# Five fp32 query/key blocks instead of four between the softmax steps of a fused encoder layer, and a new slot plan for its small products

## What is computed

```python
fox_q, fox_k, fox_v, logf, mla_q, ckv, kr = project_mixers(h, pos, w_in, b_f, g_cq, w_uq, g_ckv)
fox_o = attend(fox_q, fox_k, fox_v, ..., FOX_SCALE, 1, cum, cum)     # group A, frame-causal
mk, mv = mla_keys_values(ckv, kr, w_ukv)
mla_o = attend(mla_q, mk, mv, ..., MLA_SCALE, CHUNK)                 # group B, chunk-causal
mixed = concat([rms_norm(fox_o, g_fox_out), rms_norm(mla_o, g_mla_out)])
x = x + mixed @ w_o
x = x + cross_attention(rms_norm(x, g_mem), mem_k, mem_v) @ w_mo     # 4 heads, 256 memory tokens
x = x + (silu(hf @ w_gate) * (hf @ w_up)) @ w_down                   # hidden 2816
```

## Time and profile before

| what | value |
|---|---|
| median of 3 runs | 945.84 us (945.76 to 948.37) |
| the profiled execution | 946.38 us, its span 944.6 us |
| PE busy | 881.9 us, 93% of the span, 6186 matmuls |
| PEld busy | 839.0 us, 89% |
| DVE, ACT, POOL busy | 393.7, 382.4, 383.0 us |
| DMA | 75.46 MB, mean 80 GB/s |
| chain that ended last | PE 67%, of it L371 21%, L372 20%, L373 20% |

### The profile page before, as it was taken

One profiled execution on the slowest core, in us unless ns is written; L12 is line 12 of the kernel. 1 busy time (PEld: TensorE's weight loads), 2 busy tenths in 40 slices (PEclk: granted clock), 3 DMA queues, 4 the chain that ended last, 5 costly groups with the idle time before them and its releaser, 6 DMA issues.

```text
span 944.6 us, 15579 instructions
## 1 busy us (share of the span) xinstructions
PE 881.9 (93%) x6186; PEld 839.0 (89%) x6186; DVE 393.7 (42%) x629; ACT 382.4 (40%) x686; POOL 383.0 (41%) x195
## 2 busy tenths in 40 slices
PE   6999999889999899898798999999999998999995
PEld 6988988778888899787698999999999998999994
DVE  5255555566667755934475221222222220211213
ACT  6343565566778434455353323332322331211210
POOL 5365963535325354752033434334334432433410
PEclk9999999789999999999899999999999998999997
DMA  7333321000113233340031332232232232223202
GB/s 232 112 100 126 99 79 53 23 0 19 45 60 132 90 94 113 90 129 23 1 90 46 112 89 70 86 87 68 89 89 78 77 83 62 85 78 85 84 17 101
DMA packets 25092, 75.46 MB, mean 80 GB/s; under 512 B 2880, under 2 KB 5000, under 8 KB 24904
## 3 DMA queue, kind: packets, MB, share of 16 engines
q1 hardware_dynamic: 25040, 74.74, 26.2%
HBM read 68.20 MB, written 6.53 MB: 79 GB/s over the span
## 4 chain that ended last, share of the span: by engine, by line
PE 67%; DVE 6%; issue 4%; ACT 4%; POOL 1%; DMA 0%; DVEq 0%; ACTq 0%
PE ps L371 21%; PE ps L372 20%; PE ps L373 20%; PE ps L534 2%; PE ps L517 1%; PE ps L543 1%; PE ps L389 1%; DVE sqacc L1556 1%; DVE small L1405 1%; PE ps L397 1%; DVE ptlo L1410 1%; DVE xb L1677 1%; DVE hlo L1549 1%; ACT hhi L867 1%; POOL wlo L1688 1%
## 5 line engine op out<-in xcount | busy, mean ns | idle before, releaser
L371 PE MATMUL ps<-hhi,whi 128*128 128x288 f32 x1120 | 336.5, 300 | 19.2 <-POOL wlo L1688 9.4
L372 PE MATMUL ps<-hhi,wlo 128*128 128x288 f32 x1120 | 333.5, 298 | 0.0
L373 PE MATMUL ps<-hlo,whi 128*128 128x288 f32 x1120 | 332.9, 297 | 0.0
L1827 POOL TENSOR_TENSOR wlo<-wraw,whi 128x1024 fp32r<-128x1024 f32 (+1 forms) x68 | 161.2, 2372 | 268.8 <-ACT whi L867 268.8
L371 PEld LDWEIGHTS ps<-hhi,whi 128*128 128x128 f32 x1120 | 213.5, 191 | 21.9 <-POOL wlo L1688 9.1
L372 PEld LDWEIGHTS ps<-hhi,wlo 128*128 128x128 f32 x1120 | 212.2, 189 | 0.1
L373 PEld LDWEIGHTS ps<-hlo,whi 128*128 128x128 f32 x1120 | 212.1, 189 | 0.0
L1688 POOL TENSOR_TENSOR wlo<-wraw,whi 128x1024 fp32r<-128x1024 f32 (+1 forms) x49 | 119.5, 2445 | 201.7 <-ACT whi L867 201.3
L867 ACT ACTIVATE whi<-wraw 128x1024 fp32r<-128x1024 f32 (+1 forms) x117 | 119.2, 1023 | 137.1 <-PE ps L373 123.1
L371 PE MATMUL ps<-hidhi,whi 128*128 128x288 f32 x352 | 105.3, 299 | 3.4 <-DVE hidlo L1663 3.4
L372 PE MATMUL ps<-hidhi,wlo 128*128 128x288 f32 x352 | 105.1, 299 | 0.0
(11 more groups left out here) (238 smaller groups left out, 1468.3 us busy)
## 6 DMA issues: line engine op xcount, KB each, us to landing
wraw<-w_ff SPq DMA_DIRECT2D x44, 512.0 KB, 3.5
wraw<-w_front SPq DMA_DIRECT2D x41, 512.0 KB, 3.6
wraw<-w_down SPq DMA_DIRECT2D x16, 512.0 KB, 3.6
wraw<-w_front SPq DMA_DIRECT2D x8, 384.0 KB, 3.5
wraw<-w_down SPq DMA_DIRECT2D x8, 384.0 KB, 3.2
xs<-x_t SPq DMA_DIRECT2D x8, 288.0 KB, 5.7
xa<-x_t SPq DMA_DIRECT2D x8, 288.0 KB, 5.2
out_y<-xb SPq DMA_DIRECT2D x8, 288.0 KB, 2.3
```

The costliest lines, as they stand in the source:

```text
L371: nc.tensor.matmul(out, lh, rh, start=start, stop=False)
L372: nc.tensor.matmul(out, ll, rh, start=False, stop=False)
L373: return nc.tensor.matmul(out, lh, rl, start=False, stop=stop)
L1827: g.tensor_tensor(ffw(c, 1, 1, n)[:, 0, :], wraw[:, c % 2, 0:n], f(ffw(c, 0, 1, n)[:, 0, :]), ALU.subtract)\
```

## The change

The block K1 leaves the stretch before the loop: the loop there makes three blocks (Q0, K0, Q1), and `QK_AT` has ten entries instead of eight, so that slots 0 to 19 all carry 12 matmuls of a query/key block (before, slots 0 to 7 and 11 to 18). Everything that follows K1's place moves with it: its eviction, the casts and low parts of heads 2 and 3 (from slots 0 to 3 to slots 5 and 6), the loads of past keys, and which filler frees which weight block (`FILLER_END`). `joined(c)` moves from slot 5c + 9 to slot 5c + 10. The latent pieces are given new slots in `UQ_AT`, `KP_AT` and `V_AT`, the transposes in `RB_AT`, and the tables of ACT, DVE and POOL follow them. POOL's copies of the tables, which change alike, are left out here.

```diff
@@ -49,13 +49,13 @@
-QK_AT = (1, 3, 5, 7, 12, 14, 16, 18)
-UQ_AT = (24, 34, 43, 45, 49, 56, 60, 69)
-KP_AT = (30, 40, 51, 62)
-V_AT = ((28, 29, 32, 33, 38, 39, 42), (54, 55, 58, 59, 64, 65, 66))
-RB_AT = (22, 26, 36, 47, 67, 73, 79, 85)
+QK_AT = (1, 3, 5, 7, 9, 11, 13, 15, 17, 19)
+UQ_AT = (23, 34, 42, 44, 49, 56, 62, 66)
+KP_AT = (29, 39, 51, 60)
+V_AT = ((25, 26, 31, 32, 33, 36, 41), (46, 54, 55, 58, 59, 64, 65))
+RB_AT = (21, 27, 37, 47, 68, 72, 79, 85)
...
-FR_AT = 71
+FR_AT = 70
@@ -67,7 +67,7 @@
-FILLER_END = {15: QK_AT[1], 16: QK_AT[3], 17: QK_AT[5], 18: QK_AT[7], 19: UQ_AT[1] + 1, 20: V_AT[0][6], 21: UQ_AT[3] + 1, 22: UQ_AT[5] + 1, 23: V_AT[1][6],
+FILLER_END = {14: QK_AT[1], 15: QK_AT[3], 16: QK_AT[5], 17: QK_AT[7], 18: QK_AT[9], 19: UQ_AT[1] + 1, 20: V_AT[0][6], 21: UQ_AT[3] + 1, 22: UQ_AT[5] + 1, 23: V_AT[1][6],
@@ -461,11 +461,11 @@
-            for i in range(4):
+            for i in range(3):
...
-                    pe.wait_ge(s_vev, (2, 4, 5)[i - 1])
+                    pe.wait_ge(s_vev, (2, 4)[i - 1])
@@ -523,7 +523,7 @@
-                    pe.wait_ge(s_qkev, 4)
+                    pe.wait_ge(s_vev, 5)
@@ -554,7 +554,7 @@
-                b, half = B_QK + 4 + i // 2, i % 2
+                b, half = B_QK + 3 + i // 2, i % 2
@@ -565,7 +565,7 @@
-                    pe.wait_ge(f_lo, B_QK + 4 + i // 2 + 1)
+                    pe.wait_ge(f_lo, B_QK + 3 + i // 2 + 1)
@@ -950,17 +950,17 @@
-                    act.wait_ge(s_fev, nth(QK_AT[4 * (c // 2) - 7]) + 1)
+                    act.wait_ge(s_fev, nth(QK_AT[4 * (c // 2) - 5]) + 1)
...
-                if c < 4:
-                    act.wait_ge(s_qkev, 2 * (c // 2) + 2)
+                if c < 2:
+                    act.wait_ge(s_qkev, 2)
...
-                    act.wait_ge(s_fev, nth(QK_AT[4 * (c // 2) - 5]) + 1)
+                    act.wait_ge(s_fev, nth(QK_AT[4 * (c // 2) - 3]) + 1)
@@ -1024,10 +1024,10 @@
-            HIGH_AT = (25, 30, 39, 50, 70, 76, 82, 88)
-            QUERY_HI_AT = {6: 4, 11: 5, 16: 6, 21: 7}
-            KEY_HI_AT = {0: 2, 1: 3, 9: 4, 12: 5, 20: 6, 22: 7}
-            SPLIT_AT = {2: 17, 4: 18, 8: 19, 13: 20, 19: 21, 37: 22, 44: 23, 48: 24, 59: 25, 68: 26, 72: 27, 80: 28, 85: 29,
+            HIGH_AT = (24, 30, 40, 50, 71, 75, 82, 88)
+            QUERY_HI_AT = {9: 4, 10: 5, 17: 6, 20: 7}
+            KEY_HI_AT = {5: 2, 6: 3, 13: 4, 14: 5, 21: 6, 22: 7}
+            SPLIT_AT = {4: 17, 8: 18, 12: 19, 16: 20, 22: 21, 36: 22, 43: 23, 46: 24, 59: 25, 67: 26, 69: 27, 80: 28, 85: 29,
@@ -1360,21 +1360,21 @@
-                    dve.wait_ge(s_fev, nth(QK_AT[4 * (c // 2) - 7]) + 1)
+                    dve.wait_ge(s_fev, nth(QK_AT[4 * (c // 2) - 5]) + 1)
...
-                if c < 4:
-                    dve.wait_ge(s_qkev, 2 * (c // 2) + 2)
+                if c < 2:
+                    dve.wait_ge(s_qkev, 2)
...
-                    dve.wait_ge(s_fev, nth(QK_AT[4 * (c // 2) - 5]) + 1)
-                    dve.wait_ge(s_qk, 5 * c - 15)
+                    dve.wait_ge(s_fev, nth(QK_AT[4 * (c // 2) - 3]) + 1)
+                    dve.wait_ge(s_qk, max(5 * c - 15, 1))
...
-            for i in range(4):
+            for i in range(3):
@@ -1386,14 +1386,9 @@
-                    if p == 1:
-                        dve.wait_ge(x_klo, 2)
-                        dve.wait_ge(x_kdup, 2)
-                        dve.wait_ge(s_kst[0], 16)
...
-                    if p == 0:
-                        key_dup(0)
-                        key_dup(1)
+                    key_dup(0)
+                    key_dup(1)
@@ -1420,8 +1415,8 @@
-                    p, c = 2 + i // 4, slice(i % 2 * HT, i % 2 * HT + HT)
-                    if i % 4 < 2:
+                    p, c = (i + 6) // 4, slice(i % 2 * HT, i % 2 * HT + HT)
+                    if i % 4 >= 2:
@@ -1484,9 +1479,9 @@
-            LOW_AT = (26, 31, 40, 51, 71, 77, 83, 89)
-            QUERY_DUP_AT = {7: 4, 11: 5, 17: 6, 21: 7}
-            KEY_DUP_AT = {2: 2, 3: 3, 9: 4, 12: 5, 20: 6, 22: 7}
+            LOW_AT = (25, 31, 41, 51, 72, 76, 83, 89)
+            QUERY_DUP_AT = {9: 4, 10: 5, 17: 6, 20: 7}
+            KEY_DUP_AT = {5: 2, 6: 3, 13: 4, 14: 5, 21: 6, 22: 7}
@@ -1494,17 +1489,17 @@
-                if s >= 9 and s % 5 == 4 and s // 5 <= 16:
-                    joined(s // 5 - 1)
+                if s == QK_AT[9] + 1:
+                    dve.wait_ge(s_o, 2)
+                    v.tensor_copy(olof[:, 0, :], olof0[:, :]).then_inc(s_omove, 1)
+                if s >= 10 and s % 5 == 0 and s // 5 <= 17:
+                    joined(s // 5 - 2)
...
-                if s == QK_AT[7] + 1:
-                    dve.wait_ge(s_o, 2)
-                    v.tensor_copy(olof[:, 0, :], olof0[:, :]).then_inc(s_omove, 1)
@@ -1715,6 +1710,8 @@
+                if c == 7:
+                    pool.wait_ge(s_rb, 1)
@@ -1723,9 +1720,7 @@
-                    pool.wait_ge(f_lo, {0: 15, 2: 17, 4: 20, 6: 22}[c])
-                if c == 6:
-                    pool.wait_ge(s_rb, 1)
+                    pool.wait_ge(f_lo, {0: 15, 2: 18, 4: 20, 6: 21}[c])
@@ -1772,10 +1767,12 @@
-                    if r == 2:
-                        pool.wait_ge(s_oacc, 1)
+                    if r == 0:
+                        pool.wait_ge(s_uqlo, 1)
+                    elif r == 2:
+                        pool.wait_ge(f_lo, 23)
...
-                        pool.wait_ge(s_rb, {0: 2, 1: 3, 3: 4}[r])
+                        pool.wait_ge(s_rb, {1: 3, 3: 4}[r])
@@ -1916,25 +1913,25 @@
-            new_keys(1, s_qkev, 4)
+            new_keys(1, s_fev, nth(QK_AT[1]) + 1)
...
-            past_keys(2)
...
+            past_keys(2)
...
-            new_keys(2, s_fev, nth(QK_AT[3]) + 1)
...
-            past_keys(3)
+            new_keys(2, s_fev, nth(QK_AT[5]) + 1)
...
+            past_keys(3)
...
-            new_keys(3, s_fev, nth(QK_AT[7]) + 1)
...
+            new_keys(3, s_fev, nth(QK_AT[9]) + 1)
...
```

More of the change, by code:

```diff
@@ L1741, in _ @@
                     rest(15)
-            REST_AT = {2: 17, 4: 18, 8: 19, 13: 20, 19: 21, 37: 22, 44: 23, 48: 24, 59: 25, 68: 26, 72: 27, 80: 28, 85: 29,
+            REST_AT = {4: 17, 8: 18, 12: 19, 16: 20, 22: 21, 36: 22, 43: 23, 46: 24, 59: 25, 67: 26, 69: 27, 80: 28, 85: 29,
                        87: 30, 91: 31, 92: 32}
-            HIGH_AT = (25, 30, 39, 50, 70, 76, 82, 88)
-            QUERY_LO_AT = {6: 4, 11: 5, 16: 6, 21: 7}
-            KEY_LO_AT = {0: 2, 1: 3, 9: 4, 12: 5, 20: 6, 22: 7}
+            HIGH_AT = (24, 30, 40, 50, 71, 75, 82, 88)
+            QUERY_LO_AT = {9: 4, 10: 5, 17: 6, 20: 7}
+            KEY_LO_AT = {5: 2, 6: 3, 13: 4, 14: 5, 21: 6, 22: 7}
             RB_BUILD = (20, 24, 31, 41, 51, 70, 75, 82)
```

## The result

The changed kernel is slower: 951.49 us median (946.02 to 962.0, 20 runs); the kernel before beside it took 945.9 us (940.84 to 952.82, 20 runs). The ratio is 1.0065 with a 95% interval of 1.0042 to 1.0088. The forecast was 941.9 us: the sign is wrong, and the time lies above the range's end of 948.0.

A forecast was written before the change was run, and what follows sets the result against it. PE was taken as the bound nearly everywhere, except in parts of the attention loop with waits and a lower clock. Terms -2.5 + 2.7 - 1.2 - 1.6 - 0.8 - 0.5 = -3.9 us gave 941.9 us, range 937.5 to 948.0.

The forecast's parts named there:

- the rest of the new plan: Slots 26 to 94: the other moved latent pieces and work were costed at 0 us, ends -2 and +2.
- The start, -2.5: Before the loop to slot 2: removing K1 gains only 2.5 us of 6.46, since PE waits for POOL, then ACT.
- Slots 8 to 19, +2.7: 48 more matmuls fill every slot without gaps: +1.1 us for slots 8 to 13, +1.6 for slot 19.
- Slots 20 to `values(3)`, -1.2: From slot 20 to `values(3)`: shorter DVE queue, 7.7 us instead of 8.89, ends 6.7 and 8.9.
- `values(3)` to slot 26, -1.6: After `values(3)`: 9.4 us instead of 11.03, with half of today's loss to the lower clock, 2.5 us.
- rival 2: Slots 20 to 25: waits move with the work, clock down as long as now; sum -1.4, 944.4 us; chance 0.22.
- The joins, -0.5: Slots 26 to 94: joins one slot later lose most of their 10.9 us wait for `osum`; -0.5 us, ends 0 and -2.
- The -0.8 of the piece brought forward: Slots 26 to 94: one latent piece done earlier is missing later where PE is the bound, -0.8 us.
- Rival 3: Slots 40 to 43: DVE's queue delays `values(8)` and the clock falls; +3.0 us, 948.8 us; chance 0.19.

The follow-up runs named there:

- the change's first half alone: The change with every latent piece, factor turn, split and rest from slot 21 on put back where the kernel before has it: 941.55 us, ratio 0.9959.
- change again: The changed kernel unaltered, timed and traced once more against the kernel before: 951.04 us, ratio 1.0065.

## Why the prediction was wrong

**The failed step** is the sentence "I cost the rest of the new plan at nothing, ends -2 and +2" for slots 26 to 94. With the two small terms beside it (-0.8 and -0.5) I had slots 26 and later at -1.3 us; the profiled execution has +10.6. Putting the late places back is worth 1.0065 to 0.9959, some 10 us, and putting them alone into the kernel before costs 1.19%. The forecast of 941.9 us fits the change's first half alone, which measured 941.55; that is partly luck, since its terms missed in both directions, as below. I had looked for the plan's price in the lengths of the earlier trace rows and in which pieces move, not in what each engine's queue would hold beside which instruction of another.

**What stood in its place.** Against the kernel before, the traces put it in slots 40 to 44, 44 to 70 and 70 to 79, and some in 26 to 31. Two things undo nearly all of it behind slot 36: `hlo` of both pairs moved and the places from slot 54 on put back give 104.89 us for slots 36 to 79, where the kernel before has 103.96 and the change 113.84.

- Block 27's split and rest in slot 69, ahead of the last query rest and the factor tile, instead of 72: shown by 1.0017 to 0.995 with one edit. With the other places from slot 54 on put back as well it is 0.9938, no more than the intervals allow to be nothing, though the traces show those 3.1 us shorter over slots 44 to 79 (84.23 against 87.36). Which of them makes the 2.1 us in slots 44 to 70 wasn't run.
- `hlo` of pair 2 in slot 41, beside POOL's key rest and behind four key writes: 1.6 us in the traces (13.07 to 11.43), too little for the ratios to tell.

`hlo` of pair 1 is another matter. Moving it takes 5.1 us off slots 31 to 36 of the change, and both pairs moved give 1.0017 for 1.0065. But the kernel before has it in the same slot and spends 17.16 us there, so it is in the main a gain that both kernels leave, not a part of what the change lost. The kernel before with that edit alone wasn't run. Nor does any run move pair 1 and block 27 in the change without pair 2.

**The start, -2.5**: the first wait was right, the first scores came at 105.92 behind POOL's key part (forecast 106.5). The second was not. I had kept the landing of block 16 at 109.49, 3.0 us behind the first scores; it came 1.25 behind them:

```profile
107.17 1.06 ACT L867 ACTIVATE whi<-wraw 128x1024 fp32r<-128x1024 f32 x1 [1.66 <-DMA wraw<-w_front]
...
109.54 0.37 ACT L867 ACTIVATE probs<-ps,small 128x128 f32<-128x128 f32 x1
```

So `expo(0)` was done at 109.9, when PE at full clock would just have got there. What I had not foreseen is that the clock would fall (107.5 to 110.9, mean 0.69 over slots 0 and 1): these took 5.47 us instead of 4.0, and slot 2 began at 111.39 (forecast 112.4), so the start gave 3.5. Two misses of opposite sign, 2.5 and 1.5 us, make the difference of 1.0. In the other traces of kernels with the same start the block landed 1.2 to 1.5 us behind the first scores too, PE waited at most 0.24 us for `expo(0)`, and slot 2 began between 110.36 and 112.41.

**Slots 8 to 19, +2.7**: right. Slot 2 to slot 20 took 48.82 us, where 46.3 lay between them before (161.18 less 114.9): +2.5, no wait, full clock. In the table's first row this doesn't show, since the maxima of slot 20 were late before. Slot 20 began at 160.21, just before the 160.5 that I had named. The casts cost nothing, slot 10 included.

**Slots 20 to `values(3)`, -1.2**: 6.92 us, so -2.0. The cast in slot 20 took 0.46 us, not the 1.3 I took, so the stretch ended near its low end (6.7); `rb` was ready 3.2 us behind the slot's start (forecast 3.1).

**`values(3)` to slot 26, -1.6**: 12.44 us, so +1.4; at 0.52 over the first 9 us it is rival 2's clock. The same kernel, traced again, had the lower clock for 6.8 us instead of 10.2 in slots 20 to 26 and took 1.5 less there. The size of this term is the clock's, and it differs from one execution to the next; my ends (6.9 and 11.9) were too near for the first trace.

**The joins, -0.5**: the waits of 10.9 us did go. What that is worth depends on the places: nothing with the old ones, half a per cent with the new. The -0.8 of the piece brought forward is isolated by no run.

**Rival 3** named slots 40 to 43 and a queue of four key writes, join and `hlo`. The place was right: 1.7 us lost (13.06 for 11.37). But I priced `hlo` at 0.83 from the earlier trace rows, and the clock did not fall behind slot 42. It was a sixth of the loss. That rival's time, 948.8 us, is the nearest of all to the measured 951.49, but by a fall of the clock behind slot 42 that did not come.

## What to carry to other kernels

A plan by slots moves stands in every engine's queue, so before costing a move at nothing, list for each late slot what the engine has ahead of the item that PE waits for, and what the neighbour engine runs meanwhile. In these traces a DVE instruction that reads two tiles of SBUF had its usual price only while GpSimd rested: beside GpSimd it cost nearly its own time plus what was left of GpSimd's instruction. And an undo or a repair needs the same reading as the change: moving the split to slot 76 removed one overlap and made another, and moving `hlo` back one slot, with ACT's part, traded the overlap for a wait on ACT. Last, ask of each stall whether the kernel before has it too: the one in slots 31 to 36, the first that I found, was no part of the loss.

## What the runs showed of the hardware

`hlo` reads two SBUF tiles and takes 0.75 to 0.82 us alone. Issued while a GpSimd instruction with SBUF inputs runs, it ended 0.60 to 0.62 us after that instruction's end in each of these six cases, whatever was left of it:

| kernel, slot | GpSimd ends | hlo issued | hlo ends |
|---|---|---|---|
| before, 31 | 196.36 | 196.15 | 196.97 |
| change, 25 | 180.12 | 179.44 | 180.73 |
| change, 31 | 196.90 | 195.41 | 197.52 |
| change, 41 | 225.71 | 224.28 | 226.33 |
| change, 51 | 249.38 | 248.73 | 249.98 |
| change again, 31 | 195.66 | 194.18 | 196.27 |

GpSimd's key rest took 1.97 us beside `hlo` and 1.98 without it. So the first of the two is not slowed, and the later one stands still. It works the other way too: `rb` behind `hlo` took 1.19 us for 0.72. The join, which reads PSUM and one SBUF tile, took its usual 0.75 us in slot 25 beside the same GpSimd instruction that held `hlo` up. The Trainium skill (SBUF — State Buffer, "Who interferes with whom") states that a VectorE instruction with two SBUF inputs contends with a GpSimd instruction that reads SBUF, and that the order of issue decides which of two such instructions blocks; in the prediction I had used the section for the casts alone. The traces agree with it.

I had also not expected how much the falls of the clock weigh. Slots 31 to 36 take 11.27 us at full clock and 16.34 with a wait of 2.0 us more and 6.8 us at the lower level. And the falls differ between executions of one kernel: 10.2 and 6.8 us in slots 20 to 26 of the change's two traces.
